# Expert stage of a hybrid encoder layer: X0's turn beside A0's, the slot table's products behind A1's turn

## The chip, the cores and the metric

The kernel runs on one core of one Trainium2 chip. The metric is the device time of one execution in microseconds. A core has five engines that run their own instruction lists and wait for each other by semaphores: PE (TensorE, matrix products), DVE (VectorE), ACT (ScalarE), POOL (GpSimd) and SP (SyncE, which here only issues loads). Sixteen DMA engines move data between HBM and the on-chip memory SBUF. PE writes into eight PSUM banks of 128 x 512 float32; ACT and DVE read them.

## The reference

One layer: x (512 tokens x 1024, float32) goes through a combined projection, neighbourhood attention and a bidirectional RWKV-7, and then through a mixture of 32 experts of which each token takes 4. The change lies in the experts:

```python
def clamped_swiglu(hcat):
    gate, lin = hcat[:, :D_EXPERT], hcat[:, D_EXPERT:]
    gate = jnp.minimum(gate, SWIGLU_LIMIT)
    lin = jnp.clip(lin, -SWIGLU_LIMIT, SWIGLU_LIMIT)
    return (lin + 1.0) * (gate * jax.nn.sigmoid(SWIGLU_ALPHA * gate))
...
    def expert_block(args):
        xb, e = args
        hcat = xb @ w_up[e] + b_up[e]
        return clamped_swiglu(hcat) @ w_down[e] + b_down[e]
```

Each expert takes its rows (at most 128 in one block), multiplies them with a 1024 x 2048 and a 1024 x 1024 matrix, and adds the result, weighted, to the rows of its tokens. Products are kept at float32 precision.

## The kernel before, in words

The stages ahead of the experts (projection, mixer, router) end at about 540 us and are not touched.

**Data of an expert.** Its 12 MB of weights come in 12 *slots* of 1 MB, numbered j = 4 to 15 in the block of one expert: 4 to 7 are the second half of the up matrix (results U10, U11), 8 and 9 the first half of the down matrix (D0, D1), 10 to 13 the first half of the *next* expert's up matrix (U00, U01), 14 and 15 the rest of the down matrix. So the block of expert n already works on n + 1 in its middle. SP loads a slot into one of 6 raw buffers (`w_raw`), as soon as DVE is done with the slot 6 back.

**Splitting.** To keep float32 precision, each operand is split into a high and a low part. For a slot, ACT writes `moe_w_hi` (L2173, called hi(j) here), DVE writes `moe_w_lo` = raw - hi (L2177, lo(j)). Both live in a ring of 4 places: hi(j) waits for the load and until PE is done with slot j - 4. PE does 12 products per slot, three for each of four (hi x hi L2191, lo of the rows L2192, lo of the weights L2194), each 512 columns.

**Turning.** The rows stand with tokens on the partitions and are needed with features there. PE turns them 128 x 128 at a time, four turns to a group and a bank (`pe_turn`, L2229): X0 and X1 are the two halves of the next expert's gathered rows (`moe_x_gathered`), A0 and A1 those of this expert's activations (`moe_act_natural`). After each group ACT writes the hi part out of the bank (`take_hi`, L2234) and DVE the lo part (`take_lo`, L2240), which frees the bank.

**The slot table.** Which token stands in which row of expert n + 2 is found by DVE's comparison (`dve_sel`, L2244, `moe_slot_of_token`), four small PE products (`pe_meta`, L2221, bank M), three small DVE instructions (`dve_rows`, L2250 to L2255) and then POOL's gather (L2267) out of HBM into `moe_x_gathered`. POOL's scatter (L2276) adds an expert's results to HBM.

**Order.** Each engine's order is written out by hand: `pe_block`, `act_block`, `dve_block` and `pool_block` of one expert, in a loop over 15 pairs of experts, and one pair behind it. PE's order in a block before: slots 4, 5, A0's turn, slots 6, 7, X0's turn, slot 8, X1's turn, slot 9, slots 10, 11, A1's turn, slots 12, 13, the bias products (L2208), the table's products, slots 14, 15. Waits to know: X0's turn waits for the gather; slot 10 waits until both X halves are split; X1's turn waits until its bank is free; the table's products wait for the comparison. A table (`EXPERT_BANKS`) says which bank each result uses: U10 2, U11 3, D0 4, D1 5, U00 0, U01 1, and A0 and A1 bank 6, X0, X1 and M bank 7. A bank's users take turns in the order of the block, counted on one semaphore per bank.

## Time and profile before

| what | value |
|---|---|
| median of 3 runs | 1725.45 us (1718.86 to 1725.81) |
| the profiled execution | 1721.03 us, span 1719.3 us |
| expert stage | from about 540 us to about 1700 us |
| busy in the whole span | PE 94%, DVE 83%, ACT 64%, POOL 14% |
| granted clock of PE, mean of the span | 0.977 of 2.4 GHz |
| DMA | 472.80 MB, mean 275 GB/s |

Times are microseconds from the first instruction. An instruction's row names its line, the tile it writes and the tiles it reads. Busy times of engines overlap, and a busy engine isn't a bound by itself: a bound shows in who waits for whom. PE's products overlap in the records: each is recorded with 0.39 us though the next starts sooner, so PE's pace is read from the distance of starts.

### The profile page before, as it was taken

The page shows a single profiled execution, that of the slowest core. Times are in us where ns is not written, and L with a number is a line of the kernel's source. Part 1 is how long each engine was busy: PE and PEld are TensorE (multiplying, and loading weights), DVE is VectorE, ACT ScalarE, POOL GpSimd, SP SyncE. Part 2 cuts the span into 40 slices and gives each one's busy share as a digit, 9 for nine tenths or more (in the row PEclk, how much of TensorE's full clock was granted, in tenths as well). Part 3 has the DMA queues.
Part 4 walks back from the last instruction along what each step waited for, and adds up shares of the span by engine and source line. Part 5 has one row for each costly group of instructions (what it writes and reads, how often), then busy time and mean ns, then how long its engine had stood idle before and what let it go on. Part 6 is the DMA issues. An engine that isn't in the chain of part 4 may idle for free.

```text
span 1719.3 us, 33742 instructions
## 1 busy us (share of the span) xinstructions
PE 1620.2 (94%) x12579; PEld 1322.0 (77%) x12580; DVE 1434.0 (83%) x1555; ACT 1106.2 (64%) x1080; POOL 243.8 (14%) x200
## 2 busy tenths in 40 slices
PE   7999889889796999999999999999999999999994
PEld 6778777778675778878888878888888878878883
DVE  5585677676586899999999999999999999989995
ACT  5643525433325777777777777777777777777773
POOL 0001111010103211111211112111111112111110
PEclk9999999999896999999999999999999999999997
DMA  6232101000338999999999999999999999999994
GB/s 202 74 101 55 32 14 30 10 22 15 104 136 265 361 387 375 376 384 371 385 366 385 379 378 377 375 384 380 382 368 377 383 380 375 363 369 385 384 380 132
DMA packets 208032, 472.80 MB, mean 275 GB/s; under 512 B 18782, under 2 KB 29868, under 8 KB 207852
## 3 DMA queue, kind: packets, MB, share of 16 engines
q1 hardware_dynamic: 197579, 442.22, 69.6%
q0 software_dynamic: 9792, 27.28, 7.1%
q10 hardware_dynamic: 576, 2.10, 0.3%
q8 instruction: 64, 1.05, 0.3%
q14 instruction: 21, 0.16, 0.0%
HBM read 453.83 MB, written 26.08 MB: 279 GB/s over the span
## 4 chain that ended last, share of the span: by engine, by line
PE 56%; DMA 8%; ACT 2%; DVE 2%; issue 1%; SPq 0%; POOLq 0%; DVEq 0%; ACTq 0%
PE bank L2191 18%; PE bank L2194 17%; PE bank L2192 17%; DMA w_raw<-in_expert_w_up 6%; PE bank L2229 3%; ACT moe_w_hi L2173 2%; DVE moe_w_lo L2177 1%; PE bank L2208 0%; DMA moe_x_gathered<-hn_rows,moe_gather_rows 0%; DMA sum_rows<-moe_y,moe_scatter_rows 0%; DMA x<-sum_rows 0%; SPq L1469 0%; PE bank L2221 0%; DVE moe_x_lo L2240 0%; DVE x L2675 0%
## 5 line engine op out<-in xcount | busy, mean ns | idle before, releaser
L2177 DVE TENSOR_TENSOR moe_w_lo<-w_raw,moe_w_hi 128x2048 fp32r<-128x2048 f32 x384 | 874.3, 2290 | 81.9 <-ACT moe_w_hi L2173 77.6
L2173 ACT ACTIVATE moe_w_hi<-w_raw 128x2048 fp32r<-128x2048 f32 x384 | 736.1, 1917 | 136.8 <-PE bank L2194 104.5
L2191 PE MATMUL bank<-moe_w_hi,moe_x_hi 128*128 128x512 f32 x1024 | 407.8, 398 | 0.2 <-DVE moe_x_lo L2240 0.2
L2194 PE MATMUL bank<-moe_w_lo,moe_x_hi 128*128 128x512 f32 x1024 | 400.9, 391 | 0.0
L2192 PE MATMUL bank<-moe_w_hi,moe_x_lo 128*128 128x512 f32 x1024 | 399.8, 390 | 0.0
L2191 PEld LDWEIGHTS bank<-moe_w_hi,moe_x_hi 128*128 128x128 f32 x1024 | 192.9, 188 | 42.8 <-DVE moe_x_lo L2240 4.7
L2194 PEld LDWEIGHTS bank<-moe_w_lo,moe_x_hi 128*128 128x128 f32 x1024 | 192.8, 188 | 41.9
L2192 PEld LDWEIGHTS bank<-moe_w_hi,moe_x_lo 128*128 128x128 f32 x1024 | 193.2, 189 | 38.4
L2191 PE MATMUL bank<-moe_w_hi,moe_a_hi 128*128 128x512 f32 x512 | 208.9, 408 | 1.4 <-DVE moe_a_lo L2240 1.4
L2192 PE MATMUL bank<-moe_w_hi,moe_a_lo 128*128 128x512 f32 x512 | 200.1, 391 | 0.0
L2194 PE MATMUL bank<-moe_w_lo,moe_a_hi 128*128 128x512 f32 x512 | 199.9, 390 | 0.0
L2267 POOL DMA_INDIRECT moe_x_gathered<-hn_rows,moe_gather_rows x32 | 70.8, 2213 | 602.2 <-DVE moe_gather_rows L2255 602.2
L2194 PEld LDWEIGHTS bank<-moe_w_lo,moe_a_hi 128*128 128x128 f32 x512 | 96.2, 188 | 21.7
L2191 PEld LDWEIGHTS bank<-moe_w_hi,moe_a_hi 128*128 128x128 f32 x512 | 96.2, 188 | 19.2 <-DVE moe_a_lo L2240 1.6
L2192 PEld LDWEIGHTS bank<-moe_w_hi,moe_a_lo 128*128 128x128 f32 x512 | 96.5, 188 | 17.1
L2213 POOL COPY moe_bias_rows<-biasb 128x512 bf16 (+1 forms) x32 | 55.0, 1719 | 251.2 <-DMA sum_rows<-moe_y,moe_scatter_rows 244.5
L2234 ACT ACTIVATE moe_a_hi<-bank 128x512 fp32r<-128x512 f32 x64 | 38.4, 600 | 78.1 <-PE bank L2229 78.1
L600 PE MATMUL bank<-proj_x_hi,proj_w_hi 128*128 128x512 f32 x216 | 86.0, 398 | 2.3 <-issue 2.3
L601 PE MATMUL bank<-proj_x_lo,proj_w_hi 128*128 128x512 f32 x216 | 84.8, 393 | 0.0
L602 PE MATMUL bank<-proj_x_hi,proj_w_lo 128*128 128x512 f32 x216 | 84.7, 392 | 0.0
L288 ACT ACTIVATE proj_w_hi<-proj_w_raw 128x768 fp32r<-128x768 f32 x36 | 30.1, 844 | 68.8 <-PE bank L602 68.6
L438 DVE TENSOR_TENSOR proj_w_lo<-proj_w_raw,proj_w_hi 128x768 fp32r<-128x768 f32 x36 | 34.0, 959 | 47.2 <-ACT proj_w_hi L288 47.2
(343 smaller groups left out, 2059.9 us busy)
## 6 DMA issues: line engine op xcount, KB each, us to landing
w_raw<-in_expert_w_up SPq DMA_DIRECT2D x512, 512.0 KB, 6.9
w_raw<-in_expert_w_down SPq DMA_DIRECT2D x256, 512.0 KB
proj_w_raw<-in_w_in SPq DMA_DIRECT2D x36, 384.0 KB, 3.3
mixer_bias_table<-in_att_bias SPq DMA_DIRECT2D x16, 256.0 KB
x<-in_w_o SPq DMA_DIRECT2D x8, 512.0 KB, 6.8
sum_rows<-x SPq DMA_DIRECT2D x5, 512.0 KB, 4.5
x<-in_x ACTq DMA_DIRECT2D x4, 512.0 KB
x<-in_x SPq DMA_DIRECT2D x4, 512.0 KB, 4.1
```

The lines of the kernel that those rows point to most:

```text
L600: pe.matmul(out, w_hi[:, s, w], x_hi[:, k, :], start=(k == 0), stop=False)
L601: pe.matmul(out, w_hi[:, s, w], x_lo[:, k, :], start=False, stop=False)
L602: ins = pe.matmul(out, w_lo[:, s, w], x_hi[:, k, :], start=False, stop=(k == KD - 1))
L2173: act.activation(w_hi[:, j % RING, :], raw[:, j % RAW, :], ACT.Copy).then_inc(hi_w[j % RING], 1)
L2177: eng.tensor_tensor(w_lo[:, j % RING, :], raw[:, j % RAW, :], w_hi[:, j % RING, :].bitcast(F32), ALU.subtract)\
L2191: pe.matmul(out, s_hi[:, k, :], w_hi[:, j % RING, w], start=first, stop=False)
L2192: pe.matmul(out, s_lo[:, k, :], w_hi[:, j % RING, w], start=False, stop=False)
L2194: ins = pe.matmul(out, s_hi[:, k, :], w_lo[:, j % RING, w], start=False, stop=ends)
L2213: pool.tensor_copy(brow[:, :], biasb[:, ds(e // GRP, 1), :].rearrange("p a s -> p (a s)")).then_inc(bias_ready, 1)
L2229: ins = pe.transpose(B.tile(key)[:, P * q:P * q + P], src[:, P * k:P * k + P], ident[:, :])
L2234: act.activation(dst[:, 4 * half:4 * half + 4, :].rearrange("p k s -> p (k s)"), B.tile(key)[:, :], ACT.Copy)\
L2267: pool.indirect_dma_start(out=xg[:, :], out_offset=None, in_=hn_dram, in_offset=bass.IndirectOffsetOnAxis(ap=from_row[:, 0:1], axis=0), bo ...
```

## The change: X0's turn, the table's products, the comparison and two takes are moved

Nothing is added to or taken from the work. In `pe_block` X0's turn goes from behind slot 7 to directly behind A0's turn, ahead of slot 6. The table's products go from behind the bias products to directly behind A1's turn. For this X1 changes to bank 6, A1 to bank 7 and M to bank 6; so X0 and A0 use different banks, and so do X0 and X1. In `act_block` the take of X0 goes behind the wait for U11. In `dve_block` the comparison `moe_slot_of_token` goes from behind lo(14) to directly behind X0's `moe_x_lo`. In the last pair of experts, where X0 or M have nothing to do, `unused` counts their semaphores.

```diff
-EXPERT_BANKS = {"U10": 2, "U11": 3, "A0": 6, "X0": 7, "X1": 7, "D0": 4, "D1": 5, "U00": 0, "U01": 1, "A1": 6, "M": 7}
+EXPERT_BANKS = {"U10": 2, "U11": 3, "A0": 6, "X0": 7, "X1": 6, "D0": 4, "D1": 5, "U00": 0, "U01": 1, "A1": 7, "M": 6}
...
+        def unused(pe, B, key):
+            pe.sem_inc(B.fill_sem(key), 1)
+            pe.sem_inc(B.free_sem(key), 1)
+
         def pe_block(pe, n, e, B, it, par, nxt, nxt2):
...
                 if j == 5:
                     pe.wait_ge(actd, 2 * n + 1)
                     pe_turn(pe, B, it, (par, "A0"), an, 0)
-            if nxt:
-                pe.wait_ge(gathered, 16 * n + 32)
-                pe_turn(pe, B, it, (par, "X0"), xg, 0)
+                    if nxt:
+                        pe.wait_ge(gathered, 16 * n + 32)
+                        pe_turn(pe, B, it, (par, "X0"), xg, 0)
+                    elif B is main:
+                        unused(pe, B, (par, "X0"))
...
                     if j == 11:
                         pe.wait_ge(actd, 2 * n + 2)
                         pe_turn(pe, B, it, (par, "A1"), an, 1)
+                        if nxt2:
+                            pe_meta(pe, n + 2, e + 2, B, it, (par, "M"))
+                        else:
+                            unused(pe, B, (par, "M"))
                 biases(pe, n + 1, B, it, par, B, it + par, 1 - par)
-                if nxt2:
-                    pe_meta(pe, n + 2, e + 2, B, it, (par, "M"))
...
             split_hi(act, n, 9)
             split_hi(act, n, 10)
-            if nxt:
-                take_hi(act, B, it, (par, "X0"), x_hi, 0, hi_x)
             last = (par, "U11")
             act.wait_ge(B.fill_sem(last), B.count(it, last))
             act.sem_inc(used[3], 1)
+            if nxt:
+                take_hi(act, B, it, (par, "X0"), x_hi, 0, hi_x)
             split_hi(act, n, 11)
...
                 take_lo(dve, B, it, (par, "X0"), x_hi, x_lo, 0, hi_x, 2 * n + 3)
+            if nxt2:
+                dve_sel(dve, n + 2, e + 2, 0)
             dve_swiglu(dve, n, B, it, par, 1, 0)
...
                 lo(13, 14)
-                if nxt2:
-                    dve_sel(dve, n + 2, e + 2, 0)
             take_lo(dve, B, it, (par, "A1"), a_hi, a_lo, 1, hi_a, 2 * n + 2)
```

PE, behind slot 5 of the changed kernel's first block in the loop: A0's turn writes from `moe_act_natural`, X0's from `moe_x_gathered`; the rows L2191 to L2194 are slot products, ISA rows are waits.

```order
L2192 MATMUL bank<-moe_w_hi,moe_x_lo 128x512
L2194 MATMUL bank<-moe_w_lo,moe_x_hi 128x512
L2309 ISA
L2226 ISA
L2229 MATMUL bank<-ident,moe_act_natural 128x128 x4
L2312 ISA
L2226 ISA
L2229 MATMUL bank<-ident,moe_x_gathered 128x128 x4
L2191 MATMUL bank<-moe_w_hi,moe_x_hi 128x512
L2192 MATMUL bank<-moe_w_hi,moe_x_lo 128x512
```

In the kernel before, the 24 products of slots 6 and 7 stand between the two groups of turns; now they follow both.

PE, behind slot 11 of the changed kernel: A1's turn and the four products of the table (L2221), which before stood behind the bias products (L2208), 24 slot products later.

```order
L2328 REGISTER_ALU
L2226 REGISTER_ALU
L2229 MATMUL bank<-ident,moe_act_natural 128x128 x4
L2218 REGISTER_ALU
L2221 ISA
L2221 MATMUL bank<-meta,moe_slot_of_token 128x5
L2221 ISA
L2221 MATMUL bank<-meta,moe_slot_of_token 128x5
L2221 ISA
L2221 MATMUL bank<-meta,moe_slot_of_token 128x5
L2221 ISA
L2221 MATMUL bank<-meta,moe_slot_of_token 128x5
```

The bias products now go over directly into slot 14.

DVE, in the same block, the difference of the two: around X0's `moe_x_lo` (the L2240 row), and around lo(13) and lo(14) (the x2 row).

```order
 L2240 TENSOR_TENSOR moe_x_lo<-bank,moe_x_hi 128x512
+L2244 ISA
+L2244 TENSOR_TENSOR moe_slot_of_token<-iota,posm 128x512
 L2287 REGISTER_ALU
 L2288 TENSOR_SCALAR moe_linear_part<-bank 128x512
...
 L2177 TENSOR_TENSOR moe_w_lo<-w_raw,moe_w_hi 128x2048 x2
-L2244 ISA
-L2244 TENSOR_TENSOR moe_slot_of_token<-iota,posm 128x512
 L2238 REGISTER_ALU
 L2240 TENSOR_TENSOR moe_a_lo<-bank,moe_a_hi 128x512
```

The comparison now stands between X0's `moe_x_lo` and `moe_linear_part`, ahead of lo(11) and of X1's `moe_x_lo`.

## Rows read from the trace of the kernel before

**Rows 1.** Stretches: from:to, length, busy us (instructions) by engine, clock, DMA share, GB/s

```profile
1100.00:1200.00 100.00, 100.00 (x476) 81.77 (x475) 93.47 (x75) 77.08 (x59) 19.08 (x12) 1.00 1.04 380
```

**Rows 2.** Waits from 560 to 1700 us: us in total, times, longest

```profile
PEld bank L2229 <- DVE moe_x_lo L2240: 8.7, 8, 2.4
PEld bank L2191 <- DVE moe_x_lo L2240: 4.7, 12, 0.6
...
ACT moe_w_hi L2173 <- DMA w_raw<-in_expert_w_up: 23.9, 25, 3.2
```

**Rows 3.** Timeline of PE, a quiet expert: start, us, line, tiles, count

```profile
1039.56 0.60 PE L2229 MATMUL bank<-ident,moe_act_natural 128*128 128x128 f32 x4
...
1040.23 0.40 PE L2192 MATMUL bank<-moe_w_hi,moe_x_lo 128*128 128x512 f32 x1
...
1045.49 0.60 PE L2229 MATMUL bank<-ident,moe_x_gathered 128*128 128x128 f32 x4
...
1051.92 0.39 PE L2191 MATMUL bank<-moe_w_hi,moe_x_hi 128*128 128x512 f32 x1
...
1057.36 0.60 PE L2229 MATMUL bank<-ident,moe_act_natural 128*128 128x128 f32 x4
...
1074.81 0.60 PE L2229 MATMUL bank<-ident,moe_act_natural 128*128 128x128 f32 x4
```

**Rows 4.** Timeline of ACT, the same expert; in brackets idle time and what ended it

```profile
1043.03 1.92 ACT L2173 ACTIVATE moe_w_hi<-w_raw 128x2048 fp32r<-128x2048 f32 x1 [0.43 <-PE bank L2194]
```

**Rows 5.** Timeline of DVE, the same expert

```profile
1042.63 4.64 DVE L2177 TENSOR_TENSOR moe_w_lo<-w_raw,moe_w_hi 128x2048 fp32r<-128x2048 f32 x2 [0.61 <-ACT moe_w_hi L2173]
1047.19 0.68 DVE L2240 TENSOR_TENSOR moe_x_lo<-bank,moe_x_hi 128x512 fp32r<-128x512 f32 x1
1047.79 0.68 DVE L2288 TENSOR_SCALAR moe_linear_part<-bank 128x512 f32<-128x512 f32 x1
...
1050.77 0.68 DVE L2240 TENSOR_TENSOR moe_x_lo<-bank,moe_x_hi 128x512 fp32r<-128x512 f32 x1
...
1059.17 0.68 DVE L2244 TENSOR_TENSOR moe_slot_of_token<-iota,posm 128x512 bf16<-128x512 f32 x1
```

**Rows 6.** Timeline of ACT, DVE and PE, a disturbed expert

```profile
1008.25 1.92 ACT L2173 ACTIVATE moe_w_hi<-w_raw 128x2048 fp32r<-128x2048 f32 x1 [1.98 <-DMA w_raw<-in_expert_w_up]
...
1015.81 0.68 DVE L2240 TENSOR_TENSOR moe_x_lo<-bank,moe_x_hi 128x512 fp32r<-128x512 f32 x1
...
1016.54 0.50 PE L2191 MATMUL bank<-moe_w_hi,moe_x_hi 128*128 128x512 f32 x1
```

**Rows 7.** Chain of waits, the piece of one group of turns

```profile
1039.72 0.44 PE bank L2229 x4
```

**Rows 8.** Timeline of PE around the bias products, with the table's and without

```profile
1027.82 0.39 PE L2194 MATMUL bank<-moe_w_lo,moe_x_hi 128*128 128x512 f32 x1
1028.14 0.39 PE L2208 MATMUL bank<-moe_bias_rows,moe_bias_selector 24*128 24x512 bf16 x4
1028.47 0.25 PE L2221 MATMUL bank<-meta,moe_slot_of_token 128*128 x4
...
1028.90 0.39 PE L2192 MATMUL bank<-moe_w_hi,moe_a_lo 128*128 128x512 f32 x1
...
1665.73 0.39 PE L2208 MATMUL bank<-moe_bias_rows,moe_bias_selector 24*128 24x512 bf16 x4
...
1677.10 0.60 PE L2229 MATMUL bank<-ident,moe_act_natural 128*128 128x128 f32 x4
```

**Rows 9.** The gathers: POOL, the chain, DMA issues (us to landing), queue 0 in 1036:1039.6

```profile
1031.75 2.23 POOL L2267 DMA_INDIRECT moe_x_gathered<-hn_rows,moe_gather_rows  x1 [21.91 <-DVE moe_gather_rows L2255]
...
543.58 7.30 DMA moe_x_gathered<-hn_rows,moe_gather_rows
...
sum_rows<-moe_y,moe_scatter_rows POOLq DMA_INDIRECT x32, 9.1
...
q0 software_dynamic: 144, 0.31, 21.9%
```

## The prediction

> **What bounds the kernel now.** I read the page first: it fills PE, DVE and the DMA engines alike all through the expert stage. The stretches sharpen that: in 100 us PE is busy for 100.00, DVE for 93, ACT for 77, at a granted clock of 1.00 [rows 1]. So the question is whether PE ever waits. The waits say: hardly. From 560 to 1700 us it waited 8.7 us in all at a turn (L2229, eight times) and 4.7 us at a slot's first product (L2191, twelve times), both for DVE's `moe_x_lo` [rows 2].
>
> The timeline of a quiet expert shows why. The reader is to see one product every 0.227 us: 24 products (two slots) take 1057.36 - 1051.92 = 5.44 us. With one group of four turns ahead of them, 24 products take 1045.49 - 1039.56 = 5.93, so a group costs 0.49 us. From A0's turn to the next A0's turn pass 1074.81 - 1039.56 = 35.25 us [rows 3]. PE's own work: 144 products x 0.2267 = 32.64; four groups of turns x 0.49 = 1.96; bias and table products, 0.63 (below). That is 35.23: in a quiet expert PE doesn't wait at all. What is added on PE, or on a chain that PE waits for, is added 30 times.
>
> The nearest such chain runs from slot 6 to slot 10: slot 6's last product frees the ring place; ACT makes hi(10) (1043.03, 1.92 us) [rows 4]; DVE makes lo(10) (the pair begun at 1042.63 lasts 4.64, one alone 2.29, so the second starts at 44.98), then `moe_x_lo` of X0 at 1047.19, `moe_linear_part` at 1047.79, lo(11), and `moe_x_lo` of X1 from 1050.77 to 1051.45 [rows 5]. Slot 10 begins at 1051.92 [rows 3]. In a disturbed expert, where hi(10) waited for its load until 1008.25, X1's `moe_x_lo` ended at 1015.81 + 0.68 = 1016.49 and slot 10 began at 1016.54 [rows 6]: the handover costs 0.05. So the chain's spare time in a quiet expert is 1051.92 - 1051.45 - 0.05 = **0.42 us**. The forecast hangs on this.
>
> **The change, part by part.**
>
> *X0's turn behind A0's.* The four turns are the same work, but stand ahead of slot 6 now and no longer behind slot 7. In the chain of waits a group of four takes 0.44 us [rows 7], so slot 6 ends 0.44 later (0.49 at most). Hi(10) waits for just that, and lo(10) started 0.03 us after hi(10) ended (1043.03 + 1.92 = 1044.95) [rows 4, 5]: the chain moves by 0.44 in full. On PE itself the merger can save only what a group costs beyond its four steps, 0.49 - 0.44 = 0.05 us, and between A0's turn and slot 10 that is worth nothing if the chain is late there.
>
> *X1 in another bank.* X1's turn no longer waits for X0's `moe_x_lo` (8.7 us in eight places [rows 2]). But slot 10 waits for X1's `moe_x_lo`, which DVE makes behind X0's, linear part and lo(11). In the disturbed expert slot 10 came directly on it, 0.05 behind [rows 6]: DVE sets the time there, whether the turn between waits or not, so the wait moves from the turn to slot 10. I take 0 gained; at most the 8.7.
>
> *The comparison `moe_slot_of_token` ahead of `moe_linear_part`.* It lasts 0.68 us, as `moe_x_lo` does, and behind one of that length the next starts 0.60 after it (1047.19 to 1047.79) [rows 5]. It is the same work as before, but stood behind lo(14), off the chain, and now stands in it. A part is absorbed: from hi(10) to the end of X1's `moe_x_lo` the quiet expert takes 1051.45 - 1043.03 = 8.42, the disturbed one 1016.49 - 1008.25 = 8.24 [rows 4 to 6]; so DVE idles 0.18 in the quiet one, and 0.60 - 0.18 = 0.42 counts.
>
> Chain together: 0.44 + 0.42 = 0.86 us later, less 0.42 spare: **slot 10 starts 0.44 us later** (0.40 to 0.55) in each of some 19 quiet experts: 8.4 us. In the other 12 (the slot-10 waits of [rows 2]) the spare time is gone already. There hi(10) is late through its load (ACT waited 23.9 us for such loads, 25 times [rows 2]), so X0's 0.44 hides behind the load and the 0.60 counts: at most 7.2 us in all. Since the loads are now asked for more slowly, by 0.5 us in 35, part of the lateness goes away; I take 0.35 each, 4.2. Bounds for all twelve: -9 (the lateness goes nearly wholly) and +7.2.
>
> *ACT takes X0 after the wait for U11.* Before, X0's turn came right behind slot 7; now slot 7 itself ends 0.44 later, at the same time. DVE reads `moe_x_hi` only when lo(10) is done, later than that. Nothing gained or lost.
>
> *The table's products (L2221) behind A1's turn.* What they cost now: with them, from the bias products to A0's turn 1039.56 - 1028.14 = 11.42; without them, in the last expert but one, 1677.10 - 1665.73 = 11.37 [rows 3, 8]. So where they are they cost **0.05** us, hidden in the bias products' pass; and the two together 11.42 - 48 x 0.2267 + (1028.14 - 1027.82 - 0.227) = 0.63. Directly behind a turn the trace has none at this clock. The nearest rows: the first comes 1028.47 - 1028.14 = 0.33 behind the bias products, 0.10 more than one pass of 512 columns (0.227), and the next slot product but one 0.43 behind it (1028.90) [rows 8], where behind a turn alone that product stands 0.34 behind the last turn's start (1039.56 + 0.33 to 1040.23) [rows 3]. That makes 0.10 + 0.43 - 0.34 = 0.19. Bounds: 0.05 (hidden as now) and 0.43 (nothing hidden). I take 0.20 by those rows; less the 0.05, 0.15 x 30 = **4.5 us** (0 to 11).
>
> *The wait for the gather.* X0's turn needs the gathered rows 5.5 us earlier: at 1039.56 + 0.44 = 1040.00, 8.25 us after the gather's start at 1031.75. The trace doesn't name their landing there. The first gather, in a quieter place, landed 7.30 us after its start, and the scatters, on the same queue, land 9.1 after theirs. All 144 packets of that queue for this gather lie before 1039.6 [rows 9]. So landing lies between 7.30 and 9.1; I take 8.1 to 8.3, a little behind the last packet: the turn is just served and waits 0.07 us on the mean, 30 x 0.07 = **2 us** (0 to 0.85 x 30 = 26). Behind a wait here stand slots 6 and 7 and with them the chain. The table's products come 6 us earlier, but DVE reads them at the same place of its order, behind `moe_linear_part` of the next expert, so the gather (and the scatter behind it on POOL) starts no earlier.
>
> A rule of the Trainium skill speaks against me here. "DMA: Bandwidth & Descriptors", section "Anatomy of one DMA — SWDGE (gpsimd) path", puts most of a fixed cost of about 2 us between the last byte and the semaphore. By that the rows would land near 1039.6 + 2 = 1041.6, X0's turn would wait 1.6 us in each expert, and the sum would be 46 us higher. The first gather's 7.30 can't tell it, since its packets lay among others'; no row of before shows it.
>
> *Outside.* Everything ahead of 540 us is untouched; the first and the last experts change by tenths of a us. Where no next rows or table exist, bare semaphore counts stand in.
>
> **Sum**: 8.4 + 4.2 + 4.5 + 2 = 19.1 us. The profiled execution took 1721.03; the sum gives 1740.1. The median of the three runs (1725.45) lies 4.4 above the profiled one, the lowest 2 below; I say **1741**.
>
> **The rivals.**
>
> *A, faster: the chain holds.* If the chain grows by less than the 0.42 spare (because hi(10) didn't really wait for slot 6, or the comparison falls into a gap of DVE), what remains is the gain: X1's turn free of X0's `moe_x_lo`, up to 8.7 us, and twice 0.05 x 30 = 3 us for merged groups, against 4.5 for the table: 1714. For it: the waits at L2229 are real. Against: lo(10) starts 0.03 behind hi(10), and DVE is full from 1042.63 to 1051.45 but for 0.18 us. 0.05.
>
> *B, no change: the lateness pays.* The twelve late experts lose nearly all of their waits, because each load has 0.5 us more: 8.4 - 9 + 4.5 + 2 gives 1727. For it: the 23.9 us of waits for loads. Against: a load that is 2 us late isn't mended by 0.5. 0.10.
>
> *C, much slower: the gather is late.* If it lands as late as the scatter (9.1), X0's turn waits 0.85 in each of 30 experts, and slot 6, hi(10) and slot 10 follow: 26 instead of 2, 1764. By the Trainium skill's rule it would be 1721 + 17 + 48 = 1786. For it: the margin is at most 0.4 us behind the last packet. Against: the first landing of 7.30. 0.10.
>
> *D, the table's products stay hidden behind the turn,* and the chain is as forecast: 1736. It lies within the forecast's own range.
>
> **How the numbers follow.** Forecast with D 0.75, A 0.05, B 0.10, C 0.10. The forecast's own range: from 8.4 + 0 + 0 + 0, 1729, to 10 + 7.2 + 11 + 5, 1754; the 8 in 10 take it as it is, since B and C lie beyond its ends. A measurement here can't tell less than 0.5% (8.6 us) from no change. Slower by more: the forecast less its lowest end, and C, 0.85. Within: B and that end, 0.10. Faster: A, 0.05.
>
> **What would show it.** In the trace of the change: slot 6's second product starts 1.1 us after A0's turn (0.67 before); X1's `moe_x_lo` ends 12.8 us after A0's turn (11.9 before), and slot 10 starts 0.05 behind it (12.36 after the turn before); DVE is named for a wait at L2191 in some 30 experts, of 0.4 to 0.6 us each, and no longer at L2229; from A0's turn to the next 35.25 becomes 35.8 to 36.0; PE falls below 99% in the stretches. X0's turn would name the gather as its releaser in a few experts. I am wrong if slot 10 still starts 12.4 us after the turn (A), if X0's turn waits for the gather in most experts (C), or if the slots behind the table's products stand no later than behind a bare turn (D).

## The result and the profile after

The changed kernel takes **1736.32 us** in the median of six runs (1734.80 to 1740.61), the kernel before 1721.96 in six (1718.86 to 1725.81). The ratio is 1.0095, with an interval of 1.0078 to 1.0111: it is slower. The forecast was 1741 us, in a range of 1729 to 1754, with 0.85 on slower.

| | before | after |
|---|---|---|
| median, us | 1721.96 | 1736.32 |
| profiled execution, us | 1721.03 | 1740.35 |
| its span | 1719.3 | 1738.6 |
| first to last bias products in it | 1097.56 | 1113.90 |

The last line comes from the starts of the first and the last L2208 group on PE's timeline. Of the 19.3 us between the two profiled executions, 16.3 lie between these two groups; 2.2 came ahead of them (the first group starts at 570.34 and not at 568.17; over the profiled executions of this case it starts between 561.00 and 570.34, whatever the edit), and 0.8 behind. On the medians the difference is 14.4 us, by the ratio 16.4. The 16 us in the expert stage are what is to be explained.

**The stretch** of [rows 1] no longer shows PE at 100.00:

```profile
1100.00:1200.00 100.00, 99.19 (x473) 80.42 (x471) 90.97 (x72) 74.77 (x55) 15.69 (x11) 1.00 1.03 371
```

The granted clock is 1.00 as before. 473 products stand where 476 stood: three are missing in 100 us. In the stretch from 1300 to 1400 us PE is busy for 98.80, with 471 products.

**The waits** from 560 to 1710 us say where (us in total, times, longest):

```profile
PEld bank L2191 <- DVE moe_x_lo L2240: 27.7, 31, 3.3
...
ACT moe_w_hi L2173 <- DMA w_raw<-in_expert_w_up: 7.9, 6, 4.1
```

Against [rows 2] two lines have changed. PE now waits for DVE's `moe_x_lo` at a slot's first product in all 31 experts that have next rows (before in twelve), and nowhere at a turn. In the last of the 31 it is 0.17 us only: there is no comparison in its chain. And ACT's waits for loads have fallen from 23.9 us in 25 places to 7.9 in six: the loads have become less late. The two lines together are the story in short: a loss in each expert, and a part of it given back.

**The timeline of PE, a quiet expert** (it answers to [rows 3]):

```profile
1048.95 0.60 PE L2229 MATMUL bank<-ident,moe_act_natural 128*128 128x128 f32 x4
1049.38 0.60 PE L2229 MATMUL bank<-ident,moe_x_gathered 128*128 128x128 f32 x4
...
1050.05 0.39 PE L2192 MATMUL bank<-moe_w_hi,moe_x_lo 128*128 128x512 f32 x1
...
1061.79 0.50 PE L2191 MATMUL bank<-moe_w_hi,moe_x_hi 128*128 128x512 f32 x1 [0.40 <-DVE moe_x_lo L2240]
1062.12 0.40 PE L2192 MATMUL bank<-moe_w_hi,moe_x_lo 128*128 128x512 f32 x1
...
1067.36 0.60 PE L2229 MATMUL bank<-ident,moe_act_natural 128*128 128x128 f32 x4
1067.80 0.24 PE L2221 MATMUL bank<-meta,moe_slot_of_token 128*128 x4
...
1068.21 0.39 PE L2192 MATMUL bank<-moe_w_hi,moe_x_lo 128*128 128x512 f32 x1
...
1073.52 0.39 PE L2208 MATMUL bank<-moe_bias_rows,moe_bias_selector 24*128 24x512 bf16 x4
...
1084.88 0.38 PE L2229 MATMUL bank<-ident,moe_act_natural 128*128 128x128 f32 x2
```

The reader is to see X0's turn 0.43 us behind A0's, without a releaser in brackets: the gather wasn't waited for. Then, at slot 10, the bracket names DVE. Cut at the same four places, the two executions compare so:

| piece | before | after | difference | forecast |
|---|---|---|---|---|
| A0's turn to slot 10 | 12.36 | 12.84 | +0.48 | +0.44 |
| slot 10 to A1's turn | 5.44 | 5.57 | +0.13 | 0 |
| A1's turn to the next A0's | 17.45 | 17.52 | +0.07 | +0.15 |
| A0's turn to the next A0's | 35.25 | 35.93 | +0.68 | +0.59 |

**ACT and DVE in the same expert** (they answer to [rows 4, 5]):

```profile
1052.83 1.92 ACT L2173 ACTIVATE moe_w_hi<-w_raw 128x2048 fp32r<-128x2048 f32 x1 [0.84 <-PE bank L2194]
```

```profile
1054.78 2.29 DVE L2177 TENSOR_TENSOR moe_w_lo<-w_raw,moe_w_hi 128x2048 fp32r<-128x2048 f32 x1 [0.47 <-ACT moe_w_hi L2173]
1056.99 0.68 DVE L2240 TENSOR_TENSOR moe_x_lo<-bank,moe_x_hi 128x512 fp32r<-128x512 f32 x1
1057.59 0.74 DVE L2244 TENSOR_TENSOR moe_slot_of_token<-iota,posm 128x512 bf16<-128x512 f32 x1
1058.25 0.68 DVE L2288 TENSOR_SCALAR moe_linear_part<-bank 128x512 f32<-128x512 f32 x1
1058.85 2.28 DVE L2177 TENSOR_TENSOR moe_w_lo<-w_raw,moe_w_hi 128x2048 fp32r<-128x2048 f32 x1
1061.05 0.68 DVE L2240 TENSOR_TENSOR moe_x_lo<-bank,moe_x_hi 128x512 fp32r<-128x512 f32 x1
```

From the end of ACT's hi(10), 1054.75, on, DVE has no gap; X1's `moe_x_lo` ends at 1061.73 and slot 10 starts 0.06 behind. Hi(10) started 3.88 us after A0's turn; before it was 1043.03 - 1039.56 = 3.47. **The chain of waits** runs through just these instructions, which it did not before (start, us, what):

```profile
1049.11 0.87 PE bank L2229 x8
...
1052.83 1.93 ACT moe_w_hi L2173
1056.99 0.68 DVE moe_x_lo L2240
1057.67 0.54 DVE moe_slot_of_token L2244
1058.25 0.68 DVE moe_linear_part L2288
...
1061.05 0.69 DVE moe_x_lo L2240
1061.79 0.50 PE bank L2191
```

`moe_x_lo`, the comparison and the linear part stand in it one behind the other: the detour by ACT and DVE that the forecast drew. The 8 turns of one group take 0.87 us.

In 26 of the 31 experts X0's turn stands 0.43 or 0.44 us behind A0's. In five it stands further behind, most at 941.50 behind 940.81, 0.69 us; the five together lost 0.6 us there.

### The profile page after: what moved, and what is told of

Read it like the earlier page. It is cut to its first block, busy times and chain, and to the rows that moved or that the text cites. A ratio compares the mean times of both kernels' runs of the same rounds, so it can differ in the third digit from the quotient of the medians.

```text
span 1738.6 us, 33686 instructions
## 1 busy us (share of the span) xinstructions
PE 1630.8 (94%) x12579; PEld 1329.5 (76%) x12580; DVE 1431.8 (82%) x1555; ACT 1104.6 (64%) x1080; POOL 248.1 (14%) x200
## 4 chain that ended last, share of the span: by engine, by line
PE 50%; issue 7%; DVE 6%; ACT 4%; DMA 2%; DVEq 0%; SPq 0%; ACTq 0%; POOLq 0%
PE bank L2191 16%; PE bank L2194 15%; PE bank L2192 15%; ACT moe_w_hi L2173 3%; PE bank L2229 3%; DVE moe_x_lo L2240 2%; DVE moe_linear_part L2288 1%; DMA w_raw<-in_expert_w_up 1%; DVE moe_w_lo L2177 1%; DVE moe_slot_of_token L2244 1%; PE bank L2208 1%; DMA moe_x_gathered<-hn_rows,moe_gather_rows 0%; DMA x<-sum_rows 0%; DMA sum_rows<-moe_y,moe_scatter_rows 0%; PE bank L2221 0%
## 5 line engine op out<-in xcount | busy, mean ns | idle before, releaser
L2191 PE MATMUL bank<-moe_w_hi,moe_x_hi 128*128 128x512 f32 x1024 | 408.8, 399 | 16.1 <-DVE moe_x_lo L2240 14.9
L2194 PE MATMUL bank<-moe_w_lo,moe_x_hi 128*128 128x512 f32 x1024 | 399.8, 390 | 0.0
L2191 PEld LDWEIGHTS bank<-moe_w_hi,moe_x_hi 128*128 128x128 f32 x1024 | 192.8, 188 | 66.5 <-DVE moe_x_lo L2240 27.7
L2194 PEld LDWEIGHTS bank<-moe_w_lo,moe_x_hi 128*128 128x128 f32 x1024 | 192.7, 188 | 41.0
L2191 PE MATMUL bank<-moe_w_hi,moe_a_hi 128*128 128x512 f32 x512 | 206.7, 404 | 1.7 <-DVE moe_a_lo L2240 1.7
L2194 PE MATMUL bank<-moe_w_lo,moe_a_hi 128*128 128x512 f32 x512 | 200.4, 391 | 0.0
L2191 PEld LDWEIGHTS bank<-moe_w_hi,moe_a_hi 128*128 128x128 f32 x512 | 96.1, 188 | 27.4 <-issue 7.7
L2194 PEld LDWEIGHTS bank<-moe_w_lo,moe_a_hi 128*128 128x128 f32 x512 | 96.1, 188 | 21.5
L2213 POOL COPY moe_bias_rows<-biasb 128x512 bf16 (+1 forms) x32 | 61.5, 1921 | 267.1 <-DMA sum_rows<-moe_y,moe_scatter_rows 258.9
```

Source lines behind the costliest of these rows:

```text
L2191: pe.matmul(out, s_hi[:, k, :], w_hi[:, j % RING, w], start=first, stop=False)
L2194: ins = pe.matmul(out, s_hi[:, k, :], w_lo[:, j % RING, w], start=False, stop=ends)
L2213: pool.tensor_copy(brow[:, :], biasb[:, ds(e // GRP, 1), :].rearrange("p a s -> p (a s)")).then_inc(bias_ready, 1)
```

## The experiments

The theory to be tested: there is one spare time of 0.42 us between DVE's chain and slot 10, and X0's turn and the comparison both draw on it. Alone each should be nearly free; together they cost. In numbers: the turn moves hi(10) by 0.41, the comparison adds 0.66, DVE had 0.18 of idle time within the chain and 0.42 behind it, so 0.47 should be left over, and 0.48 was measured. The rivals: that one of the two costs by itself, that the bank table or ACT's order does it, or that PE's own work has grown. Each kernel was timed in five rounds beside the kernel before; the ratio with its interval is what counts, and it isn't the quotient of the two medians.

| label | median, us | before beside | ratio, interval | A0's turn to slot 10 | period |
|---|---|---|---|---|---|
| e1_comparison_off_chain | 1725.09 | 1720.55 | 1.0023, 1.0009 to 1.0037 | 12.28 | 35.43 |
| e2_comparison_in_chain | 1723.51 | 1720.55 | 1.0000, 0.9988 to 1.0013 | 12.42 | 35.46 |
| e3_x0_turn_only | 1722.49 | 1720.55 | 1.0009, 0.9997 to 1.0022 | 12.27 | 35.31 |
| e4_table_behind_a1_only | 1719.76 | 1720.55 | 0.9990, 0.9974 to 1.0006 | 12.36 | 35.34 |
| e5_pe_pad | 1725.72 | 1721.36 | 1.0025, 1.0011 to 1.0040 | 12.76 | 35.65 |
| e6_linear_part_out_of_chain | 1729.49 | 1721.36 | 1.0040, 1.0023 to 1.0058 | 12.28 | 35.60 |
| e7_shorter_chain | 1719.87 | 1721.36 | 0.9985, 0.9970 to 1.0000 | 12.36 | 35.34 |
| e8_act_order_as_before | 1737.14 | 1719.90 | 1.0099, 1.0083 to 1.0116 | 12.84 | 35.95 |
| e9_comparison_twice | 1758.08 | 1721.36 | 1.0197, 1.0174 to 1.0220 | 13.44 | 36.56 |
| e10_banks_only | 1720.66 | 1719.90 | 1.0006, 0.9993 to 1.0020 | 12.36 | 35.27 |
| e11_x0_turn_and_comparison | 1733.98 | 1719.90 | 1.0085, 1.0068 to 1.0102 | 12.84 | 35.87 |

The last two columns are read off PE's timeline: the first in a quiet expert, the second as the median over the distances from one A0's turn to the next, without the first and the last of the 31. In the kernel before it is 35.27, in the changed one 35.95. In e1, e3 and e6 few experts are quiet, since X0's turn is often late: the medians of the first column there are 12.45, 12.38 and 12.52; in the others they are within 0.01 of the value shown.

### The two moves, each alone and both together

**e2, the comparison alone**, in the kernel before:

```diff
                 take_lo(dve, B, it, (par, "X0"), x_hi, x_lo, 0, hi_x, 2 * n + 3)
+            if nxt2:
+                dve_sel(dve, n + 2, e + 2, 0)
             dve_swiglu(dve, n, B, it, par, 1, 0)
...
-                if nxt2:
-                    dve_sel(dve, n + 2, e + 2, 0)
```

> The kernel before with only the comparison moved into the chain, directly behind X0's moe_x_lo. Theory: 0.66 us later (the next instruction stood 1.26 behind moe_x_lo in the changed kernel, 0.60 in the one before), less 0.18 absorbed and 0.42 spare: X1's moe_x_lo ends 12.38 us after A0's turn and slot 10 starts at 12.43, 0.07 later, plus about 0.14 us because PE has stopped (its first products behind a stop are slower). That is 0.2 us in 30 experts, and 0.6 in those with a late load, less what the loads catch up: +3 to +9 us. Rival 1 (the comparison alone makes the whole loss, whatever PE does): +14. Rival 2 (it costs nothing while X0's turn stands behind slot 7): within 2 us of before.

Its timeline of DVE and PE:

```profile
1041.78 0.49 PE L2229 MATMUL bank<-ident,moe_act_natural 128*128 128x128 f32 x3
...
1050.01 0.74 DVE L2244 TENSOR_TENSOR moe_slot_of_token<-iota,posm 128x512 bf16<-128x512 f32 x1
1050.67 0.68 DVE L2288 TENSOR_SCALAR moe_linear_part<-bank 128x512 f32<-128x512 f32 x1
...
1053.47 0.68 DVE L2240 TENSOR_TENSOR moe_x_lo<-bank,moe_x_hi 128x512 fp32r<-128x512 f32 x1
...
1054.20 0.50 PE L2191 MATMUL bank<-moe_w_hi,moe_x_hi 128*128 128x512 f32 x1
```

The comparison holds DVE for 0.66 us (1050.01 to 1050.67). Slot 10 starts 12.42 behind the turn, 0.06 later than before and 0.05 behind X1's `moe_x_lo`: the spare time is used up and exceeded by those 0.06. The waits:

```profile
PEld bank L2191 <- DVE moe_x_lo L2240: 10.1, 29, 1.0
...
ACT moe_w_hi L2173 <- DMA w_raw<-in_expert_w_up: 7.5, 6, 4.0
```

These are waits of the weight loads, which run ahead of the products; slot 10 itself is only 0.06 late. The period is 0.19 longer (that 0.06, and the restart that is treated below), 30 x 0.19 = 5.7 us, yet the ratio is 1.0000, at most 1.0013, which is 2.2 us; the medians stand 3.0 apart. Between the first and the last bias products the profiled execution took 2.2 us more than that of before. So most of the 5.7 us didn't show, where 3 to 9 were expected. What pays for it is read from the second line: 7.5 us of waits for loads instead of 23.9 [rows 2].

**e3, X0's turn alone**, in the kernel before (banks and table as before):

```diff
                     pe_turn(pe, B, it, (par, "A0"), an, 0)
-            if nxt:
-                pe.wait_ge(gathered, 16 * n + 32)
-                pe_turn(pe, B, it, (par, "X0"), xg, 0)
+                    if nxt:
+                        pe.wait_ge(gathered, 16 * n + 32)
+                        pe_turn(pe, B, it, (par, "X0"), xg, 0)
...
-            if nxt:
-                take_hi(act, B, it, (par, "X0"), x_hi, 0, hi_x)
...
             act.sem_inc(used[3], 1)
+            if nxt:
+                take_hi(act, B, it, (par, "X0"), x_hi, 0, hi_x)
```

> The kernel before with only X0's turn moved behind A0's, and ACT's take of X0 behind the wait for U11 as in the change; banks as before. Theory: the chain moves by 0.41 us (lo(10) 5.83 instead of 5.42 after A0's turn), 0.18 is absorbed and the rest is within the spare 0.42, so slot 10 starts at 12.28, PE gains the 0.08 us that two groups of turns in a row cost less than two apart: 30 x 0.08 = 2.4 us faster, less if loads are then later: -3 to +2. Rival 1 (X0's turn is the cost): +6 or more. Rival 2 (the gather is late for it): X0's turn names the gather in most experts, +5 or more.

```profile
1038.00 0.60 PE L2229 MATMUL bank<-ident,moe_act_natural 128*128 128x128 f32 x4
...
1049.43 0.69 DVE L2240 TENSOR_TENSOR moe_x_lo<-bank,moe_x_hi 128x512 fp32r<-128x512 f32 x1
...
1050.27 0.40 PE L2191 MATMUL bank<-moe_w_hi,moe_x_hi 128*128 128x512 f32 x1
```

X1's `moe_x_lo` ends at 1050.12, so 0.10 of the 0.42 is left, beside the handover of 0.05. Slot 10 comes 12.27 after the turn: without a wait the merged groups save 0.09 us, and quiet experts follow each other in 35.20. The median is 35.31, since in 10 of 31 experts X0's turn came late behind A0's, by up to 0.51 us and 2.0 in all; the waits of PE name the gather for two of them. The time is the same within its interval. So what X0's turn costs alone is the risk of a late gather, more than its place in the chain.

**e11, both**, in the kernel before: the edits of e2 and e3 and nothing else.

> The kernel before with X0's turn behind A0's (and ACT's take behind U11) and the comparison in the chain, both together; banks and the table's products as before. Alone they gave +0.1% and 0.0%. Theory (both draw on one spare time of 0.42 us, which holds for one of them and not for two): slot 10 at 12.84, about 0.14 us more for PE's restart behind the wait, 35.8 to 35.9 us from turn to turn, +11 to +15 us: 1732 to 1736. Rival (the loss comes from the banks or from the table's products behind A1's turn): the sum of the two alone, +2 us.

Its PE at slot 10 (A0's turn at 1042.20), and its waits:

```profile
1042.20 0.60 PE L2229 MATMUL bank<-ident,moe_act_natural 128*128 128x128 f32 x4
...
1055.04 0.50 PE L2191 MATMUL bank<-moe_w_hi,moe_x_hi 128*128 128x512 f32 x1 [0.40 <-DVE moe_x_lo L2240]
```

```profile
PEld bank L2191 <- DVE moe_x_lo L2240: 25.6, 31, 1.1
...
ACT moe_w_hi L2173 <- DMA w_raw<-in_expert_w_up: 5.8, 4, 3.7
```

12.84 and 31 waits, as in the changed kernel; the ratio is 1.0085 where the two alone have 1.0000 and 1.0009. So the two moves together make nearly all of the 1.0095, and neither does it alone: what decides is their sum against one spare time. This rules out that one move is dear by itself, and it needs neither the banks nor the table's products.

### The rest of the change: little in it

**e10, the banks alone**: X1 6, A1 7, M 6 and `unused`, in the kernel before.

```diff
-... "A0": 6, "X0": 7, "X1": 7, "D0": 4, "D1": 5, "U00": 0, "U01": 1, "A1": 6, "M": 7}
+... "A0": 6, "X0": 7, "X1": 6, "D0": 4, "D1": 5, "U00": 0, "U01": 1, "A1": 7, "M": 6}
```

> The kernel before with only the banks of the change (X1 and M in bank 6, A1 in 7, and the bare counts for them in the last pair). Theory: X1's turn no longer waits for X0's moe_x_lo in the experts with late loads, but slot 10 then waits for X1's moe_x_lo the longer: the waits of before (8.7 us at a turn, 4.7 at a slot) come together at the slot's line, and the time is that of before within 2 us. Rival A of the prediction (the turns' waits are a loss of their own): 5 us or more faster.

```profile
PEld bank L2191 <- DVE moe_x_lo L2240: 7.3, 9, 2.6
...
ACT moe_w_hi L2173 <- DMA w_raw<-in_expert_w_up: 18.5, 26, 4.0
```

The wait at the turn [rows 2] is gone, and slot 10 has taken over a part of it: the two lines of before sum to 13.4 us, this one is 7.3. Each is one execution, and the ratio says no change.

**e4, the table's products alone** behind A1's turn, in the kernel before (the comparison goes only as far as it must, ahead of lo(13)):

```diff
                         pe_turn(pe, B, it, (par, "A1"), an, 1)
+                        if nxt2:
+                            pe_meta(pe, n + 2, e + 2, B, it, (par, "M"))
                 biases(pe, n + 1, B, it, par, B, it + par, 1 - par)
-                if nxt2:
-                    pe_meta(pe, n + 2, e + 2, B, it, (par, "M"))
...
-                lo(13, 14)
                 if nxt2:
                     dve_sel(dve, n + 2, e + 2, 0)
+                lo(13, 14)
```

> The kernel before with only the table's four products moved behind A1's turn (and the comparison ahead of lo(13), off the chain, so that it is there in time); banks as before. Theory: between A1's turn and the bias products 0.135 us more, behind them 0.055 less: 0.08 us in 30 experts, +2.4 us (0 to +5). Rival (the 0.15 of my prediction, or more): +4.5 us or more. No wait of the table's products for the comparison.

The period grows by 0.07 to 0.08 us (35.27 to 35.34), or 2.3 us in all; the time doesn't move (0.9990, at most 1.0006), and ACT's waits for loads are 15.3 us in 14 places.

**e8, ACT's order as before**, in the changed kernel: the take of X0 goes back ahead of the wait for U11.

> The changed kernel with ACT's take of X0 back ahead of the wait for U11. Theory: DVE reads moe_x_hi of X0 only behind lo(10), so it isn't waited for and nothing changes: slot 10 at 12.84 after A0's turn, 35.95 us from turn to turn, the time of the changed kernel within 3 us (1733 to 1740). Rival (ACT's new order held hi(11) or the take up and is part of the loss): 1731 or less.

Slot 10 at 12.84, period 35.95, 1.0099 against the changed kernel's 1.0095: no effect of this part shows.

### Single costs, on the chain and on PE

**e9, the comparison twice** in the changed kernel, the first time into a tile that nobody reads:

```diff
             if nxt2:
+                dve.tensor_tensor(again[:, :, :], iota[:, ds(0, P)].unsqueeze(1).to_broadcast([P, NT, P]),
+                                  posm[:, :, ds(e + 2, 1)].to_broadcast([P, NT, P]), ALU.is_equal)
                 dve_sel(dve, n + 2, e + 2, 0)
```

> The changed kernel with the comparison done twice in its new place (the first time into a tile that nobody reads). Theory: the chain is bound everywhere and has no spare time, so the 0.60 to 0.66 us count in full: slot 10 at 13.44 to 13.50 after A0's turn, 36.55 to 36.6 us from turn to turn, +18 to +20 us against the changed kernel: 1754 to 1757. Rival (DVE's total work or another slack takes a part): under +10.

DVE's timeline (its line numbers are one higher):

```profile
1063.21 0.74 DVE L2387 TENSOR_TENSOR moe_comparison_again<-iota,posm 128x512 bf16<-128x512 f32 x1
1063.87 0.68 DVE L2245 TENSOR_TENSOR moe_slot_of_token<-iota,posm 128x512 bf16<-128x512 f32 x1
1064.47 0.68 DVE L2289 TENSOR_SCALAR moe_linear_part<-bank 128x512 f32<-128x512 f32 x1
```

The second comparison costs its 0.60 in full: slot 10 goes from 12.84 to 13.44, the period from 35.95 to 36.56, PE's waits from 27.7 to 45.6 us, and the ratio from 1.0095 to 1.0197, which is 17.5 us of 1721; 30 x 0.60 is 18.0. The medians, of two sets of runs, stand 21.8 apart, and 1758.08 lies 1 us above what was expected. X0's turn is late in 8 experts here, by 3.8 us in all, 2.4 of it in one, so not all of the difference is the chain. Still, past the spare time what is added to this chain costs about in full, and no give-back shows: the load waits are 8.3 us in six places, as the changed kernel's 7.9.

**e5, four more turns on PE**, in the kernel before, behind X0's turn:

```diff
                 pe_turn(pe, B, it, (par, "X0"), xg, 0)
+                pe.wait_ge(B.free_sem((par, "D0")), B.before(it, (par, "D0")))
+                for q in range(4):
+                    pe.transpose(B.tile((par, "D0"))[:, P * q:P * q + P], xg[:, P * q:P * q + P], ident[:, :])
```

> The kernel before with four more turns in each expert, directly behind X0's turn, into the bank of D0 ahead of its first use; their result is not used. Pure PE time: 0.49 us in 31 experts, 15.2 us; from A0's turn to the next 35.74 us. Theory (weight loads are the second bound, close behind PE, and late only while PE asks every 35.25 us): with 0.5 us more for each MB x 12 the waits of ACT for loads fall from about 20 us to under 10 and the roughly 8 us that PE lost behind them come back, so the time rises by 5 to 10 us only. Rival (late loads are accidents that a slower pace doesn't mend): +13 to +16.

A0's turns stand at 1074.88 and 1110.52, 35.64 us apart. Four turns behind others cost 0.40 us and not 0.49. This is work of PE itself, in every expert, with no chain in it: 30 x 0.40 = 12.0 us. The medians rose by 4.4 only, a little less than expected (the ratio's interval is 1.9 to 6.9 us), while ACT's waits for loads fell to 10.3 us in six places. In the one profiled execution the stretch from the first to the last bias products grew by 7.9 us, from 1097.56 to 1105.46. So between 4 and 8 of the 12 us came back, and that doesn't depend on which wait is lengthened. That the loads are the second bound, just behind the first, is read from their waits; no run changed the loads alone.

### Attempts at a faster version

**e1, the changed kernel with the comparison off the chain** (ahead of lo(13)):

```diff
                 take_lo(dve, B, it, (par, "X0"), x_hi, x_lo, 0, hi_x, 2 * n + 3)
-            if nxt2:
-                dve_sel(dve, n + 2, e + 2, 0)
             dve_swiglu(dve, n, B, it, par, 1, 0)
...
                 dve_to_row(dve, n + 1, 1 - par, n)
+                if nxt2:
+                    dve_sel(dve, n + 2, e + 2, 0)
                 lo(13, 14)
```

> The changed kernel with one thing undone: the comparison moe_slot_of_token stands behind this expert's second activations, ahead of lo(13), and no longer between X0's moe_x_lo and moe_linear_part. Theory (the chain from slot 6 to slot 10): the chain loses the 0.60 us of the comparison and has its spare time back, so slot 10 starts about 12.28 us after A0's turn, from A0's turn to the next pass about 35.25 us, and the time is that of the kernel before within 4 us (1718 to 1727). Rival 1 (X0's turn ahead of slot 6 is the cost, since it holds hi(10) up by 0.44 us): slot 10 keeps at least 0.3 us of its delay, time 1730 or more. Rival 2 (the table's products behind A1's turn cost 0.15 us or more): 4 us or more above before, with slot 10 at 12.3.

```profile
PEld bank L2191 <- DVE moe_x_lo L2240: 12.3, 31, 2.6
...
PEld bank L2229 <- DMA moe_x_gathered<-hn_rows,moe_gather_rows: 1.3, 4, 0.7
```

Slot 10 is back at 12.28 in a quiet expert, and three quarters of the loss are gone (1.0023 of 1.0095). What stays, 1.0023, has two causes on the rows: the table's 0.08 in each period, and X0's turn, which in 18 of 31 experts now comes later than 0.43 behind A0's, 3.7 us in all; the waits name the gather.

**e6, the linear part off the chain instead**: in the changed kernel `moe_linear_part` goes behind X1's `moe_x_lo`, the comparison stays.

```diff
                 dve_sel(dve, n + 2, e + 2, 0)
-            dve_swiglu(dve, n, B, it, par, 1, 0)
             lo(11)
...
                 take_lo(dve, B, it, (par, "X1"), x_hi, x_lo, 1, hi_x, 2 * n + 4)
+            dve_swiglu(dve, n, B, it, par, 1, 0)
+            if nxt:
                 lo(12)
```

> The changed kernel, the comparison left in its new place, but moe_linear_part moved out of the chain instead, behind X1's moe_x_lo. Theory (what counts is the length of the chain, whichever instruction is in it): lo(11) starts 9.3 us after A0's turn, X1's moe_x_lo ends at 12.19, slot 10 starts at 12.28, from turn to turn 35.25 to 35.3; time 1722 to 1727, as with the comparison off the chain. Rival (the comparison itself hurts, for example by holding POOL or its own reads up): slot 10 stays at 12.8 and the time at 1736.

```profile
PEld bank L2229 <- issue: 5.9, 10, 1.7
PEld bank L2229 <- DMA moe_x_gathered<-hn_rows,moe_gather_rows: 3.4, 8, 1.0
```

This missed: 1729.49, above the range that was expected. The chain is short enough (12.28), but X0's turn is late in 22 of 31 experts, up to 1.6 us and 8.4 in all; the longest of these waits stand in the two lines above. POOL and PE of the worst stretch:

```profile
1068.14 2.25 POOL L2267 DMA_INDIRECT moe_x_gathered<-hn_rows,moe_gather_rows  x1 [21.80 <-DVE moe_gather_rows L2255]
```

```profile
1075.92 0.60 PE L2229 MATMUL bank<-ident,moe_act_natural 128*128 128x128 f32 x4
1077.96 0.65 PE L2229 MATMUL bank<-ident,moe_x_gathered 128*128 128x128 f32 x4 [1.44 <-DMA moe_x_gathered<-hn_rows,moe_gather_rows]
```

The gather starts 7.78 us before A0's turn, as it does in the changed kernel (1041.19 and 1048.95: 7.76), but the turn, for which the bracket names the gather, can run only 9.82 after the start, where in the changed kernel 8.19 was enough. So the gather isn't asked for later; it lands later. Its last packet ended 9.40 us after its start, where in the changed kernel it was 6.97; the first packets came at 5.09 and 4.60. So it is its packets that take longer. That these waits make up the 7 us is read from the rows, and why the packets take longer here is open: no run changed the gather alone.

**e7, what stayed promising**: the changed kernel's banks and table, X0's turn back behind slot 7 (and ACT's take with it), the comparison ahead of lo(13), the linear part behind X1's `moe_x_lo`.

```diff
-                    if nxt:
-                        pe.wait_ge(gathered, 16 * n + 32)
-                        pe_turn(pe, B, it, (par, "X0"), xg, 0)
...
+            if nxt:
+                pe.wait_ge(gathered, 16 * n + 32)
+                pe_turn(pe, B, it, (par, "X0"), xg, 0)
...
-            if nxt2:
-                dve_sel(dve, n + 2, e + 2, 0)
-            dve_swiglu(dve, n, B, it, par, 1, 0)
             lo(11)
...
+            dve_swiglu(dve, n, B, it, par, 1, 0)
...
+                if nxt2:
+                    dve_sel(dve, n + 2, e + 2, 0)
                 lo(13, 14)
```

> A try for a version faster than both: the changed kernel with X0's turn back behind slot 7 and ACT's take of X0 as before, the comparison off the chain (ahead of lo(13)), and moe_linear_part behind X1's moe_x_lo. The banks of the change and the table's products behind A1's turn stay. In a quiet expert slot 10 stays bound by PE at 12.36; in an expert with a late load the chain is 0.60 us shorter, and X1's turn no longer waits. Theory: 35.33 us from turn to turn (the table's 0.08 more), late experts lose 0.6 us less: 1716 to 1720, 1 to 5 us below before. Rival (DVE has no room for lo(12) and lo(13) then and they come late): 1722 or more.

```profile
PEld bank L2191 <- DVE moe_x_lo L2240: 4.1, 3, 2.0
```

It has the lowest ratio of all, 0.9985 (0.9970 to 1.0000), which is not surely faster than the kernel before, but 1% faster than the changed one. PE waits for `moe_x_lo` in three experts only; what bounds it is PE's own work, 35.34 us per expert.

## Why the prediction was right

**The chain: right, within 0.04 us.** The forecast had X1's `moe_x_lo` end 12.8 us after A0's turn and slot 10 start 0.05 behind it; it ended 12.78 behind and slot 10 came 0.06 later. It rested on three numbers: the spare time of 0.42 (e3 alone fits into it, e2 alone goes 0.06 beyond it), the turns' 0.44 (hi(10) is 0.41 later) and the comparison's 0.60, which was 0.66: behind `moe_x_lo` it holds DVE 0.06 longer than the linear part does. That makes the 0.04 between 0.44 and 0.48: 0.06, and 0.03 less from the turns, and 0.01 of handover.

**A term was missing: PE's restart.** The sum took slots 10 and 11 as 5.44 us; after the wait they take 5.57. The second product stands 0.33 behind the first (1061.79 to 1062.12) instead of 0.227; that is 0.10, and the next products at 0.23 make up the rest. So a wait of PE in this kernel costs 0.13 beyond itself, 4 us over 31 experts. Its size is the same in the changed kernel and in e11; what in PE makes it was not looked into. The trace of before had it already, in the disturbed expert of [rows 6], from slot 10 to A1's turn:

```profile
1016.54 0.50 PE L2191 MATMUL bank<-moe_w_hi,moe_x_hi 128*128 128x512 f32 x1
...
1022.12 0.60 PE L2229 MATMUL bank<-ident,moe_act_natural 128*128 128x128 f32 x4
```

That is 5.58 instead of 5.44, and twelve experts of before take 5.50 or more. The forecast read the handover in that expert and not the pace behind it.

**The table's products: the right sign, half the size.** The forecast took 0.15 net, 4.5 us. The slot's second product does stand later behind them, 0.85 behind the turn's start (1067.36 to 1068.21) where behind a bare turn it is 0.67 [rows 3]: that is 0.18 where the forecast had 0.19. But 0.05 of it is made up over the rest of the slots (A1's turn to the bias products is 6.16, before 6.03: the products cost 0.13 there), and 0.06 is saved behind the bias products (11.36, before 11.42). The net is 0.07, where the forecast had 0.15, and e4 has the same 0.07 to 0.08 by itself: 2.3 us of longer periods instead of 4.5.

**The banks and ACT's order: right, at 0** (e10, e8). The wait that the new bank removes moves in part from the turn to slot 10, and what is gone of it doesn't show in the time.

**The gather: near enough.** The forecast had it just in time, with 2 us lost. X0's turn came late in five experts, by 0.6 us in all and 0.26 at most. The rows of a usual expert:

```profile
1041.19 2.23 POOL L2267 DMA_INDIRECT moe_x_gathered<-hn_rows,moe_gather_rows  x1 [19.36 <-DVE moe_gather_rows L2255]
```

And queue 0 in 1045:1048.4 (packets, MB, share):

```profile
q0 software_dynamic: 144, 0.31, 26.0%
```

All 144 packets are there, and X0's turn ran unwaited at 1049.38, 8.19 us after the gather's start and 1.2 us behind the end of the last packet (1048.16). The Trainium skill ("DMA: Bandwidth & Descriptors", "Anatomy of one DMA — SWDGE (gpsimd) path") puts most of about 2 us there. This trace doesn't agree: it is at most 1.2 us, and in the late expert of e6, where PE did wait for the gather, X0's turn began at 1077.96, 0.4 us behind the last packet (1077.54). The 1.6 us of waiting in each expert that the forecast worked out by the Trainium skill's rule did not come, and rival C fell. How thin the margin is, e1 and e6 show: where the experts come a little faster, X0's turn does wait.

**The late experts: this term failed.** The step was "a part of the lateness goes away; I take 0.35 each, 4.2": a give-back of 12 x 0.09, about 1 us. The rows now: each period is 0.68 longer than before (35.27 to 35.95 in the median). But what single experts took above the median period, over the 29 periods between the first and the last, fell from 7.2 us in all to 1.2: **6.0 us came back** between these two executions. Of these, about 1.5 are restarts, of the experts that waited before as well. How much of the rest is the chance of one execution is open: e10, with the period of before and the same time, has 3.5 us where before has 7.2. This was rival B's mechanism, which had been given 0.10 with the argument that a load 2 us late isn't mended by 0.5 us. One expert's perhaps isn't. But every expert is longer now, and the loads have that time in each of them, those ahead of a late one too; that this is the way is argued from the waits. The same shows in e2 (5.7 us of longer periods, at most 2.2 of them in the ratio) and in e5 (12.0 us of work for 4.4), with load waits down to 7.5 and 10.3 us. B failed in its total: it gave back 9 us where 6.0 came, and the loss per expert, 0.68, came in all of them.

**Why the total came out nonetheless.** In the experts 16.3 us were measured against a forecast of 19.1. From the one to the other, term by term over 31 periods: the chain +1.2 (0.48 for 0.44), the restart +4.0, the table -2.3, the gather -2.0 (a median period has no wait for it), the give-back -4.9 (6.0 for 1.1); that makes 15.1. The 1.2 left over lie in the first period (37.82 before, 40.45 after, so 2.0 more than the median grew) and the last (35.19 in both, so 0.7 less). So two errors of 4 to 5 us stood against each other: a cost that was not seen, and a give-back that was seen and held too small. That they nearly cancel is luck. With either error alone the time would still have lain in the forecast's range, which is therefore no proof of its terms. The median of 1736.3 happens to be rival D's number; D's condition, a table at no cost, is met by half.

Rival A fell at the first row: slot 10 starts 12.84 after the turn, not 12.4. One sign came only in part: PE was to fall below 99% in the stretches, and it is 99.19 in one and 98.80 in the other.

## What to carry to other kernels

Two moves that each fit, or nearly fit, into a chain's spare time can be dear together: each alone cost 0.0 to 0.1% here, both 0.85%. Add up everything that a change puts on the path between two points of the bounding engine, against the one spare time there, before putting any of it at nothing. Where a second bound lies just behind (here the loads), a small cost in every pass is partly given back, so that 12 us of plain work cost 4 to 8; beyond it, each tenth costs about in full, and a wait costs a little more than it lasts. The price of a wait can stand in the trace of before, in the few passes that do wait: look there.

## What the runs showed of the hardware

- PE needs about 0.13 us to get back to its pace after a wait of some tenths: two slots took 5.57 us instead of 5.44, the second product coming 0.33 and not 0.227 behind the first. In the disturbed expert of the kernel before it was 5.58.
- Groups of turns cost less behind each other: four alone 0.49 us [rows 3], eight in a row 0.87 in the chain, and four added to a group 0.40 (e5).
- The comparison into bf16 holds DVE for 0.66 us behind `moe_x_lo`, but for 0.60 behind another comparison (e9); `moe_linear_part`, into float32, holds it for 0.60.
- Four products of 5 columns cost 0.05 to 0.06 us in the bias products' shadow (11.42 against 11.37 and 11.36) and 0.13 behind a turn (6.16 against 6.03); there the second product behind them was 0.18 late, and PE made up 0.05 of it over the following slots.
- Behind the last packet of a gather it took 0.4 us until X0's turn began (e6: 1077.54 to 1077.96).
